# Another order of the mixer's steps in a two-block kernel on one core

## The reference

```python
proj = h @ w_in
aq, ak, av, dqkv, dz, db, da = jnp.split(proj, IN_SPLITS, axis=-1)
attn_out = dilated_attention(aq, ak, av)                 # 8 heads of 64
dqkv = jax.nn.silu(causal_short_conv(dqkv, conv_w))      # dq, dk, dv: 4 heads of 128
g = -jnp.exp(A_log) * jax.nn.softplus(da + dt_bias)
beta = jax.nn.sigmoid(db)
o = gated_delta_rule(dq, dk, dv, g, beta)                # chunks, a triangular solve
o = rms_norm(o, dn_norm_w) * jax.nn.silu(dz)             # the gate
return jnp.concatenate([attn_out, dn_out], axis=-1) @ w_out
```

## Time and profile before

| | us |
|---|---|
| median of 3 runs | 2166.76 |
| lowest and highest run | 2165.75, 2167.95 |
| the profiled execution | 2158.39 |
| its span, first to last instruction | 2156.6 |
| TensorE busy | 2085.1 (97%) |
| VectorE busy | 978.5 (45%) |
| ScalarE busy | 327.6 (15%) |
| mean granted TensorE clock | 0.993 |

### The profile page before, as it was taken

The page is one execution under the profiler, slowest core; times in us unless marked ns, Lnnn a source line. Parts: engine busy times, 40 slices in busy tenths (PEclk is TensorE's granted clock), DMA queues, the critical chain, the costliest instruction groups (busy, mean ns, idle before and its releaser), DMA issues.

```text
span 2156.6 us, 24182 instructions
## 1 busy us (share of the span) xinstructions
PE 2085.1 (97%) x9733; PEld 1151.7 (53%) x9740; DVE 978.5 (45%) x1573; ACT 327.6 (15%) x730; POOL 48.3 (2%) x30
## 2 busy tenths in 40 slices
PE   6999999999999999999999899999999999999999
PEld 3858633333333333333223456877884648868874
DVE  1485444333333333333223245744776267626684
ACT  1132110000010000000000112311110113311110
POOL 0002000000000000000000002000000011000000
PEclk9999999999999999999999999999999999999999
DMA  9558199999999999999999835324442634244441
GB/s 371 213 202 344 46 363 409 429 427 427 427 429 426 428 427 428 427 428 427 428 428 427 306 120 194 137 80 156 156 157 98 213 120 165 97 137 148 146 160 55
DMA packets 132916, 593.53 MB, mean 275 GB/s; under 512 B 9246, under 2 KB 65742, under 8 KB 104650
## 3 DMA queue, kind: packets, MB, share of 16 engines
q1 hardware_dynamic: 132810, 592.01, 69.4%
HBM read 590.91 MB, written 3.18 MB: 275 GB/s over the span
## 4 chain that ended last, share of the span: by engine, by line
PE 80%; DMA 12%; DVE 4%; ACT 2%; issue 1%; POOL 0%; SPq 0%; POOLq 0%; DVEq 0%
PE bank L1604 23%; PE bank L673 21%; DMA ring<-in_w_dram 11%; PE bank L683 8%; PE bank L2733 6%; PE bank L2696 3%; PE bank L1745 2%; PE bank L934 2%; PE bank L2711 2%; PE bank L1585 2%; PE bank L3086 1%; PE bank L1621 1%; DMA ring<-in_w_ada_dram 1%; DVE arena L1269 1%; PE bank L2647 1%
## 5 line engine op out<-in xcount | busy, mean ns | idle before, releaser
L1604 PE MATMUL bank<-ring,arena 128*64 128x512 f32 x2304 | 510.4, 594 | 13.9 <-DMA ring<-in_w_dram 12.2
L673 PE MATMUL bank<-wide,ring 128*128 128x256 f32 x2368 | 516.3, 380 | 2.8 <-ACT wide L2970 2.6
L673 PEld LDWEIGHTS bank<-wide,ring 128*128 128x128 f32 x2368 | 450.3, 191 | 67.4 <-issue 6.1
L1604 PEld LDWEIGHTS bank<-ring,arena 128*64 128x64 f32 x2304 | 160.8, 137 | 353.4 <-issue 319.8
L1245 DVE TENSOR_SCALAR arena<-bank 128x512 f32<-128x512 f32 x32 | 22.1, 692 | 378.1 <-PE bank L1604 378.1
L683 PE MATMUL bank<-ring,wide 128*128 128x512 f32 (+2 forms) x384 | 151.2, 554 | 0.0
L2393 DVE SCALAR_TENSOR_TENSOR arena<-bank,arena 128x254 f32<-128x254 f32 (+1 forms) x176 | 76.6, 477 | 84.7 <-ACT arena L2537 83.2
L683 PEld LDWEIGHTS bank<-ring,wide 128*128 128x128 f32 x384 | 72.6, 190 | 75.1 <-issue 71.8
L1249 DVE RECIPROCAL arena<-arena 128x512 f32<-128x512 f32 x32 | 107.3, 3353 | 1.1
L1421 ACT ACTIVATE arena<-arena 128x512 f32<-128x512 f32 x32 | 20.1, 629 | 494.8 <-DVE arena L1245 494.8
L1604 PE MATMUL bank<-wide,arena 128*64 128x512 f32 x392 | 89.0, 595 | 0.7 <-ACT arena L1425 0.7
(11 more groups left out here) (515 smaller groups left out, 1967.6 us busy)
## 6 DMA issues: line engine op xcount, KB each, us to landing
ring<-in_w_dram SPq DMA_DIRECT2D x144, 2048.0 KB, 26.5
wide<-in_w_dram SPq DMA_DIRECT2D x24, 2048.0 KB, 27.3
arena<-in_w_dram SPq DMA_DIRECT2D x22, 2048.0 KB, 29.4
ring<-in_w_up_dram SPq DMA_DIRECT2D x44, 1024.0 KB, 7.4
ring<-in_w_in_dram SPq DMA_DIRECT2D x21, 2048.0 KB, 8.4
ring<-in_w_ada_dram SPq DMA_DIRECT2D x12, 2048.0 KB, 8.9
ring<-in_w_down_dram SPq DMA_DIRECT2D x10, 2048.0 KB, 7.9
ring<-in_w_out_dram SPq DMA_DIRECT2D x6, 2048.0 KB, 8.5
```

Source lines behind the costliest of these rows:

```text
L673: ins = pe.matmul(B.bank(name, j)[:, i * T:(i + 1) * T], w[:, k, (first + i) * P:(first + i + 1) * P], hT[:, k, :], start=(k == 0), stop=( ...
L1604: ins = pe.matmul(bank[g * SLOTS:(g + 1) * SLOTS, :], lhsT, rhs[:, g * CH:(g + 1) * CH], start=start, stop=stop)
```

## The change

- The gate's product `z` is computed after both score tiles and the transposes of q and k (`tm`), no longer between `v` and `ab`. The load of `ab`'s weights moves ahead of that of `z`.
- On ScalarE the copies of `tm` go between the exponentials of the two score tiles, and exp(-z) after the copies of `t0` (whose source lay in `normw[0]`) and the decays. On VectorE the gate's silu moves behind `e_mat`.
- `gc`, `row` and `fm` follow `t0` and precede `o0`: `values_t` is split into `turn_t` and `weigh_t`. ScalarE's decays, copies of `fm` and exponentials of the tables are functions of their own (`decays_s`, `features_s`), ahead of the copies of `t1`. VectorE takes squares before the second count, and scaling and tables before the divisions of both attention tiles.
- The four bf16 products ahead of `kk` are gone.

```diff
@@ -95,9 +95,9 @@
     p = Plan()
-    for name, n in (("hT", 4), ("ag0", 1), ("ad0", 1), ("qk", 4), ("convT", 1), ("rel", 1), ("dq", 6), ("v", 2), ("z", 2), ("ab", 1),
-                    ("s0", 2), ("s1", 4), ("ag1", 1), ("tm", 4), ("t0", 2), ("o0", 1), ("gc", 1), ("row", 2),
-                    ("t1", 4), ("o1", 1), ("tv", 2), ("fm", 4), ("kk", 2), ("kq", 2), ("aT", 2), ("ag2", 1),
+    for name, n in (("hT", 4), ("ag0", 1), ("ad0", 1), ("qk", 4), ("convT", 1), ("rel", 1), ("dq", 6), ("v", 2), ("ab", 1),
+                    ("s0", 2), ("s1", 4), ("tm", 4), ("z", 2), ("ag1", 1), ("t0", 2), ("gc", 1), ("row", 2), ("fm", 4),
+                    ("o0", 1), ("t1", 4), ("o1", 1), ("tv", 2), ("kk", 2), ("kq", 2), ("aT", 2), ("ag2", 1),
                     ("p2", 4), ("p4", 2), ("zz", 4), ("xx", 4)):
@@ -399,10 +399,9 @@
         ada_loads(0)
-        order = [("qk", 1, 0), ("qk", 3, 1), ("dq", 1, 3), ("dq", 3, 4), ("dq", 5, 5), ("v", 1, 2), ("z", 1, 6)]
+        order = [("qk", 1, 0), ("qk", 3, 1), ("dq", 1, 3), ("dq", 3, 4), ("dq", 5, 5), ("v", 1, 2), ("ab", 0, 7), ("z", 1, 6)]
         for nm, i, cc in order:
-            load1(CH, A["w_in"][0, :, cc * CH:(cc + 1) * CH], (nm, i))
-        load1(2 * DH, A["w_in"][0, :, 7 * CH:IN1], ("ab", 0))
+            load1(2 * DH if nm == "ab" else CH, A["w_in"][0, :, cc * CH:min((cc + 1) * CH, IN1)], (nm, i))
         ada_loads(1)
@@ -613,6 +612,10 @@
             turn_t(pe, B, S, jobs, qt, call, buf, flag)
+            weigh_t(pe, B, jobs, qt, val, PT)
+        def weigh_t(pe, B, jobs, qt, val, PT):
             pe.wait_ge(*B.room(jobs[2]))
@@ -797,6 +800,12 @@
             v.wait_ge(S["e_mat"], 2)
+            for tt in range(TT):
+                v.wait_ge(S["zx"], tt + 1)
+                e = normw[0][:, tt * DW:(tt + 1) * DW]
+                then(v.tensor_scalar(e, e, 1.0, None, ALU.add))
+                then(v.reciprocal(e, e))
+                then(v.tensor_tensor(dz[:, tt, :], dz[:, tt, :], e, ALU.mult))
@@ -867,20 +876,26 @@
+        def decays_s(act):
+            act.wait_ge(*B.taken("gc"))
+            act.activation(egc, gcum, ACT.Exp)
+            act.activation(erem[:, 0, :], sp_a[:, 0, :], ACT.Exp).then_inc(S["gexp"], 1)
+        def features_s(act):
+            for j in range(4):
+                act.wait_ge(*B.ready("fm", j))
+                act.activation(tile4((QTn, KTn)[j // 2], j % 2), b4("fm", j), ACT.Copy).then_inc(B.free("fm", j), 1)
+            act.wait_ge(*B.taken("row", 1))
+            act.activation(Am, Am, ACT.Exp, scale=-1.0)
+            act.activation(DTm, DTm, ACT.Exp).then_inc(S["dmat"], 1)
         def delta_s(act):
...
                 act.activation(tile4(Vt, j), b4("tv", j), ACT.Copy).then_inc(B.free("tv", j), 1)
-            act.wait_ge(*B.taken("gc"))
-            act.activation(egc, gcum, ACT.Exp)
-            act.activation(erem[:, 0, :], sp_a[:, 0, :], ACT.Exp).then_inc(S["gexp"], 1)
-            act.wait_ge(*B.taken("row", 1))
-            act.activation(Am, Am, ACT.Exp, scale=-1.0)
-            act.activation(DTm, DTm, ACT.Exp).then_inc(S["dmat"], 1)
-            for j in range(4):
-                act.wait_ge(*B.ready("fm", j))
-                act.activation(tile4((QTn, KTn)[j // 2], j % 2), b4("fm", j), ACT.Copy).then_inc(B.free("fm", j), 1)
             for j in range(2):
@@ -926,6 +941,12 @@
+        def features_t(pe):
+            for j in range(4):
+                pe.wait_ge(S["kqn"], j // 2 + 1)
+                four_t(pe, "fm", j, lambda out, u: pe.transpose(out, (Qt, Kt)[j // 2][:, u, :], ident), j % 2)
         def delta_t(pe):
@@ -938,11 +959,6 @@
                 four("tv", j, lambda out, u: pe.transpose(out, dT[:, 8 + u % 4, (u // 4) * P:(u // 4 + 1) * P], ident), j)
-            for j in range(4):
-                pe.wait_ge(S["kqn"], j // 2 + 1)
-                four("fm", j, lambda out, u: pe.transpose(out, (Qt, Kt)[j // 2][:, u, :], ident), j % 2)
-            pe.wait_ge(*B.room("kk"))
-            keep_running(pe, B.bank("kk"), 4)
             for j in range(4):
@@ -2933,22 +2949,16 @@
-            for tt in range(TT):
-                v.wait_ge(S["zx"], tt + 1)
-                e = normw[0][:, tt * DW:(tt + 1) * DW]
-                then(v.tensor_scalar(e, e, 1.0, None, ALU.add))
-                then(v.reciprocal(e, e))
-                then(v.tensor_tensor(dz[:, tt, :], dz[:, tt, :], e, ALU.mult))
             soft_v(v, then)
...
             decay_v(v, then)
-            for qt in range(TT):
-                count_v(v, then, S, qt, qt, c(f"dil{qt}"), expo[qt], den[qt])
+            count_v(v, then, S, 0, 0, c("dil0"), expo[0], den[0])
             squares_v(v, then)
+            count_v(v, then, S, 1, 1, c("dil1"), expo[1], den[1])
+            scaled_v(v, then)
+            rows_v(v, then)
             result_v(v, then, B, S, jobs1[0], 0, att[:, 0, :], den[0], flag="attn_p")
-            rows_v(v, then)
-            scaled_v(v, then)
             result_v(v, then, B, S, jobs1[1], 1, att[:, 1, :], den[1], flag="attn_p")
@@ -2994,20 +3004,23 @@
             out_of_psum(act, "v", 2, lambda j: av[:, j, :])
+            act.wait_ge(*B.ready("ab"))
+            act.activation(ab, split(B.bank("ab")[:, 0:16], 2), ACT.Copy).then_inc(B.free("ab"), 1)
+            soft_s(act)
+            exps_s(act, S, 0, 0, AHD ** -0.5, expo[0], amax[0], den[0])
+            turned_qk_s(act)
+            exps_s(act, S, 1, 1, AHD ** -0.5, expo[1], amax[1], den[1])
             for j in range(TT):
...
                 act.activation(dz[:, j, :], B.bank("z", j)[:], ACT.Copy).then_inc(B.free("z", j), 1)
+            ada_rows_s(act, 1)
+            turned_s(act, B, jobs1[0], 0, PT)
+            decays_s(act)
+            for j in range(TT):
                 act.wait_ge(*B.taken("z", j))
                 act.activation(normw[0][:, j * DW:(j + 1) * DW], dz[:, j, :], ACT.Exp, scale=-1.0).then_inc(S["zx"], 1)
-            act.wait_ge(*B.ready("ab"))
-            act.activation(ab, split(B.bank("ab")[:, 0:16], 2), ACT.Copy).then_inc(B.free("ab"), 1)
-            soft_s(act)
-            for qt in range(TT):
-                exps_s(act, S, qt, qt, AHD ** -0.5, expo[qt], amax[qt], den[qt])
-            ada_rows_s(act, 1)
-            turned_qk_s(act)
-            turned_s(act, B, jobs1[0], 0, PT)
+            features_s(act)
             turned_s(act, B, jobs1[1], 1, PT)
@@ -3045,13 +3058,15 @@
                 n += 1
-            for nm in ("v", "z"):
+            def rows_of(nm, n):
                 w, landed = w1_slot(n)
...
                     token_major(pe, B, nm, tt, lambda k: hT[:, k, tt * P:(tt + 1) * P], lambda k: split(w, KT)[:, k, :], KT)
-                n += 1
-            w, landed = w1_slot(n)
+            rows_of("v", n)
+            w, landed = w1_slot(n + 1)
             pe.wait_ge(*landed)
@@ -3060,18 +3075,20 @@
             ins.then_inc(B.full("ab"), 1)
-            n += 1
             for qt in range(TT):
...
                          lambda hd: qkT[64 * (hd % 2):64 * (hd % 2) + 64, 4 + hd // 2, 0:P * (qt + 1)])
+            turned_qk_t(pe)
+            rows_of("z", n + 2)
             ada_rows_t(pe, 1)
-            turned_qk_t(pe)
-            for qt in range(TT):
-                values_t(pe, B, S, jobs1[qt], qt, qt, lambda hd, kt: av[:, kt, hd * 64:(hd + 1) * 64], expo[qt], PT,
-                         flag="attn_p")
-                if qt == 0:
-                    rows_t(pe)
+            value = lambda hd, kt: av[:, kt, hd * 64:(hd + 1) * 64]
+            turn_t(pe, B, S, jobs1[0], 0, 0, expo[0], "attn_p")
+            rows_t(pe)
+            features_t(pe)
+            weigh_t(pe, B, jobs1[0], 0, value, PT)
+            turn_t(pe, B, S, jobs1[1], 1, 1, expo[1], "attn_p")
+            weigh_t(pe, B, jobs1[1], 1, value, PT)
             delta_t(pe)
```

## The result

| | before | changed |
|---|---|---|
| median of the runs, us | 2166.26 (6 runs, 2160.24 to 2167.95) | 2152.08 (6 runs, 2151.31 to 2154.75) |
| profiled execution, us (span) | 2158.39 (2156.6) | 2151.87 (2150.0) |
| mean granted clock of the profiled execution | 0.993 | 0.994 |
| ratio of the runs | | 0.995, 95% interval 0.9936 to 0.9965 |

Between the profiled executions it is 6.5.

A forecast was written before the change was run, and what follows sets the result against it. TensorE was taken as the bound, with 80% of the chain (DMA 12%). -3.64 + 0.6 + 0.1 - 1.7 = -4.6 us took the profiled 2158.39 to 2153.8; with 8.4 carried over, 2162.1, range 2158.8 to 2166.9.

The forecast's parts named there:

- the difference is carried over: Whole kernel: the median stays 8.4 us above the profiled execution, so 2153.8 becomes 2162.1.
- Waits ahead of `o0`, `fm` and `kk`, -3.64: TensorE in the reordered stretch: three waits vanish, -0.90, -0.87 and -1.87 us, the last including the bf16 products.
- step 2: Wait ahead of `fm` for VectorE's scaling: goes, -0.87 us, covered by `z` and `ag1`; uncovered, at most back.
- step 5: Gate's silu on VectorE: moved behind `e_mat` it costs +0.1 us; its removal ahead of the softening gives nothing.
- The new wait ahead of `o1`, +0.6: TensorE waits for ScalarE's copies of `t1`, now behind the tables' exponentials: +0.6 us, bounds 0 and 1.2.
- The late identity, +0.1: VectorE adds the identity 0.35 us later, ahead of `zz`; 0.28 of that is slack, so +0.1 us.
- The clock, -1.7: Second low-clock stretch, 3.4 us behind the `o0` wait, goes: -1.7 us; first, 6.8 us at `ab` and scores, stays.
- rival two: First low-clock stretch, at `ab` and scores, loses half of its 6.8 us: -6.3 in all, 2160.4 us; chance 0.14.
- The rule of the Trainium skill: Transposes don't count as busy for the clock: low stretch in `fm` to `tv`, gain 2.9 instead of 4.6 us.

The follow-up runs named there:

- all_but_z: Changed kernel with the gate's product, copies, exponentials and silu back in their old place: 2163.33 us, ratio 1.0009 to before.
- z_split: Changed kernel with tile 0 of the gate's product put back between `v` and `ab`: 2155.21 us, 1.9 above the changed kernel beside it.
- before_again: The kernel before, run again with no edit: median 2163.59 us, ratio 1.0015 to the same kernel beside it.
- z_only: Changed kernel with decays, tables and `fm` back in the old order and the four bf16 products restored: 2158.48 us, ratio 0.9984 to before.
- with_bf16: Changed kernel with the four bf16 products ahead of `kk` put back: 2155.35 us, 2.0 above the changed kernel beside it.
- best: copies_first plus the gate's first silu tile before the second division and the router's 1-column products ahead of a wait: 2148.53 us, ratio 0.9934 to before.
- copies_first: Changed kernel with ScalarE's copies of `t1` ahead of the exponentials of the tables: 2150.89 us, ratio 0.9938 to before.
- best_again: The kernel of best run once more beside the changed kernel: 2149.32 us, ratio 0.9937, 4.0 below the changed kernel.
- before_filled: The kernel before with 8 unread bf16 products ahead of `o0` and 8 instead of 4 ahead of `kk`: 2160.84 us, ratio 0.9990 to before.
- all_but_z_filled: all_but_z with 32 bf16 products in the wait ahead of `fm`: 2165.32 us.

## Why the prediction was wrong

Its direction was right, and so was each wait it took away; the size was not. The step that failed is the last of the sum, "the difference is carried over". It put 8.4 us between the profiled execution and the median. In the changed kernel that distance is 0.2 (2152.08 - 2151.87): 8.2 of the 10.0 us by which 2162.1 was missed. The profiled execution itself was forecast at 2153.8 and took 2151.87. Step by step:

1. Waits ahead of `o0`, `fm` and `kk`, -3.64: they went, as written, and with them 0.5 us around `fm` that I had not counted. But if the cover by `z` were gone, I wrote, the wait of step 2 would "at most be back", 0.87 us. In all_but_z it is 7.36.

2. The length that needs this cover I did not see. It is the 21.2 us chain from `z` to `o0` on VectorE and ScalarE. I had read the chain's shares for the whole span, where TensorE has 80%, and only single waits in the reordered stretch. "Taking it away there gives nothing", of the gate's silu at the head of this chain (step 5), is right or wrong by the execution. The first softening (the first row is before, then the changed kernel, then z_split):

```profile
142.60 1.28 DVE L529 TENSOR_TENSOR normw<-bank,con 128x512 f32<-128x512 f32 x2
```
```profile
128.56 1.29 DVE L528 TENSOR_TENSOR normw<-bank,con 128x512 f32<-128x512 f32 x2 [0.98 <-PE bank L590]
```
```profile
133.80 1.29 DVE L528 TENSOR_TENSOR normw<-bank,con 128x512 f32<-128x512 f32 x2 [1.42 <-PE bank L590]
```

With the silu ahead it starts 6.4 us behind the start of `ab`, in before, before_again and all_but_z. Without it, 5.2 us behind in the changed kernel and z_only, where the first low stretch is short, but 6.2 to 6.4 in z_split, with_bf16 and best, where it is long and the scores themselves come late. So the silu's place costs 1.2 us or next to nothing; in the profiled execution of before the stretch was long. No run moves the silu alone.

3. The new wait ahead of `o1`, +0.6: 0.81, in its range, and put down to the step named; copies_first removes it. The late identity, +0.1: 0.24.

4. The clock, -1.7: the second low stretch went, worth that. The first was shorter as well, by 3.4 us, and `ab` and scores by 1.4: what rival two, at 0.14, says. But the runs don't show that the change does this. The first stretch is 3.4 us in the unchanged kernel too (before_again), and 6.8 with the new order of `v`, `ab` and scores in with_bf16, best and best_again; in the three profiles of the changed kernel it is 3.4. Between two profiles this 1.4 is luck until more is known. The rule of the Trainium skill weighed there ("TensorE: Matmul & The Clock Gate", "Part 4: PE-mode transpose") would have put a low clock into `fm` to `tv`: the row from 155 to 172 us is at 1.00, and the same steps are at 1.00 in the two further profiles. Without the cover it did come, in all_but_z, but with a wait of 7 us, which the rule does not need.

With these, 3.64 + 0.5 + 1.7 + 1.4 - 0.8 - 0.24 = 6.2 of the 6.4 us between the two profiles. Without the 1.4 it is some 5 us, by this estimate, and the forecast of 4.6 was near it.

5. "The difference is carried over": I took the 8.4 us for a constant. It was the distance of two groups, and the change takes away the upper one. What the runs show for it: behind the wait ahead of `o0` a long execution of before has 10.3 us at half clock and not 3.4; with that wait filled (before_filled) or nearly gone (z_only), no run took more than 2161.9 us; and of the changed kernel's 25 none is in the upper group. In the first group's terms the forecast is 2159.2 - 4.6 = 2154.6 against 2152 to 2153 measured.

What stays open: what puts an execution of before into the one or the other group. In the two profiles it goes with the first low stretch: long there, short wait and short second stretch; short there, long wait and long second one. The chain from `z` to `o0` has the same length in both, so the wait follows from it. Two profiles do not show that this holds for all 84. Open too is what makes the stretch at the router's products 6.8 or 10.3 us, worth 1.6, in kernels that have the same steps there.

## What to carry to other kernels

Read the chain of waits inside the stretch that a change touches, not its shares over the span: an engine that is 97% busy can still be waiting for another there, and then making it faster only makes it wait. A step moved behind others is worth what it covers; undo it alone to see that. When the profiled execution lies outside the runs beside it, compare their clocks before carrying a difference over: a change can remove one group of executions. And before a low-clock stretch of another length is put down to a change, look for both lengths in several executions of one kernel.

## What the runs showed of the hardware

- The same program took 2159.2 us (median of 48 executions) or 2166.2 (36) on one core, parted by a mean granted clock of 0.993 to 0.997 or 0.990 to 0.992.
- Right behind the 512-column products, `ab`'s 8-column products and the scores had 3.4 or 6.8 us at 1.2 GHz without any idle time of TensorE, either length in kernels with the same steps there.
- A wait of 0.90 us in front of 64-column products went with 3.4 us at 1.2 GHz, one of 2.47 us with 10.3, and one of 7.36 with 13.7. But waits of 0.87 and 1.00 us (before), 0.81 (changed) and 1.52 (z_split) had 1.00 around them: the length of the wait alone does not decide it.
- Transposes, 64-column and 128-column float32 products, with one wait of 0.81 us among them, ran at 2.4 GHz for 17 us.
- bf16 products that nothing reads kept the clock at 1.00 in the waits they filled, and in before_filled behind them too. In all_but_z_filled 6.8 us at half clock came behind the next wait, of 1.52 us.
